# Attention outputs from split values and probabilities in fp32r, with sinks written by ScalarE

## The reference

```python
z = h @ w_in                                  # qa ka va | qb kb vb | forget gates
# sliding window, per head
m = max(max(s), sink); e = exp(s - m)
oa = (e / (sum(e) + exp(sink - m))) @ v
# forgetting, per head: F = cumsum(log sigmoid(gate))
s = q @ k.T * scale + F_q - F_k               # causal
ob = softmax(s) @ v
h = LN1(alpha * h + concat(oa, ob) @ w_o)
h = LN2(alpha * h + relu(h @ w_up)**2 @ w_down)
h = h + sigmoid(h @ w_pg + b_pg) * (p @ w_pe)
```

## Time and profile before

| | us |
|---|---|
| median of 3 runs (lowest, highest) | 2954.06 (2953.28, 2956.42) |
| the profiled execution | 2956.46 |
| its span | 2954.9 |
| PE busy | 2835.8 (96%) |
| DVE busy | 1244.1 (42%) |
| ACT busy | 856.9 (29%) |
| POOL busy | 120.6 (4%) |

### The profile page before, as it was taken

One profiled execution on the slowest core, in us unless ns is written; L12 is line 12 of the kernel. 1 busy time (PEld: TensorE's weight loads), 2 busy tenths in 40 slices (PEclk: granted clock), 3 DMA queues, 4 the chain that ended last, 5 costly groups with the idle time before them and its releaser, 6 DMA issues.

```text
span 2954.9 us, 51431 instructions
## 1 busy us (share of the span) xinstructions
PE 2835.8 (96%) x21021; PEld 2760.4 (93%) x21021; DVE 1244.1 (42%) x1759; ACT 856.9 (29%) x1377; POOL 120.6 (4%) x190
## 2 busy tenths in 40 slices
PE   7799999999899889999999999999999999998998
PEld 6688899999899889999999999999999999997998
DVE  7544443434634373333333333333333333355732
ACT  4344343434522162212222221222122112213511
POOL 0200121111100000000000000000000000000000
PEclk8899999999999999999999999999999999999999
DMA  4110122222122122222222222222222222222231
GB/s 166 46 36 29 59 85 79 74 73 81 62 65 77 64 80 79 86 80 86 86 76 82 86 86 86 86 73 86 87 79 86 79 86 81 83 74 63 87 110 52
DMA packets 65270, 230.72 MB, mean 78 GB/s; under 512 B 9280, under 2 KB 10176, under 8 KB 64576
## 3 DMA queue, kind: packets, MB, share of 16 engines
q1 hardware_dynamic: 57312, 211.31, 22.2%
q0 software_dynamic: 6160, 15.41, 1.6%
q10 hardware_dynamic: 1616, 1.18, 0.1%
HBM read 217.71 MB, written 10.16 MB: 77 GB/s over the span
## 4 chain that ended last, share of the span: by engine, by line
PE 92%; DVE 3%; issue 2%; ACT 2%; DMA 1%; ACTq 0%; DVEq 0%; POOL 0%; POOLq 0%
PE tile L354 81%; PE misc L519 3%; PE misc L354 3%; PE misc L499 1%; PE misc L463 1%; PE misc L462 1%; ACT w_hi L705 1%; DMA sv<-in_swa_cv 1%; DVE stat L1107 0%; PE misc L441 0%; PE tile L553 0%; PE misc L502 0%; PE misc L467 0%; DVE st L1041 0%; DVE acc L1035 0%
## 5 line engine op out<-in xcount | busy, mean ns | idle before, releaser
L354 PE MATMUL tile<-x_hi,w_hi 128*128 128x288 f32 (+1 forms) x4000 | 882.4, 302 | 37.5 <-DVE x_lo L1098 12.7
L354 PE MATMUL tile<-x_hi,w_lo 128*128 128x288 f32 (+1 forms) x4000 | 856.9, 296 | 0.0
L354 PE MATMUL tile<-x_lo,w_hi 128*128 128x288 f32 (+1 forms) x4000 | 856.6, 296 | 0.0
L354 PEld LDWEIGHTS tile<-x_hi,w_hi 128*128 128x128 f32 (+1 forms) x4000 | 640.3, 189 | 66.2 <-issue 54.8
L354 PEld LDWEIGHTS tile<-x_lo,w_hi 128*128 128x128 f32 (+1 forms) x4000 | 643.8, 189 | 1.2
L354 PEld LDWEIGHTS tile<-x_hi,w_lo 128*128 128x128 f32 (+1 forms) x4000 | 643.6, 189 | 1.3
L705 ACT ACTIVATE w_hi<-w_raw 128x1024 fp32r<-128x1024 f32 x394 | 406.3, 1052 | 637.5 <-PE tile L354 618.0
L1025 DVE TENSOR_TENSOR w_lo<-w_raw,w_hi 128x1024 fp32r<-128x1024 f32 x394 | 474.7, 1222 | 214.7 <-ACT w_hi L705 214.6
L354 PE MATMUL tile<-hid_hi,w_hi 128*128 128x288 f32 x2048 | 437.2, 295 | 7.9 <-DVE acc L1321 7.9
L354 PE MATMUL tile<-hid_lo,w_hi 128*128 128x288 f32 x2048 | 437.4, 294 | 0.0
L354 PE MATMUL tile<-hid_hi,w_lo 128*128 128x288 f32 x2048 | 434.5, 293 | 0.0
(11 more groups left out here) (216 smaller groups left out, 1956.5 us busy)
## 6 DMA issues: line engine op xcount, KB each, us to landing
w_raw<-in_w SPq DMA_DIRECT2D x394, 512.0 KB, 3.6
acc<-in_x SPq DMA_DIRECT2D x4, 1152.0 KB, 9.5
out_y<-st POOLq DMA_DIRECT2D x16, 288.0 KB, 2.6
out_fox_v<-v_t POOLq DMA_DIRECT2D x8, 288.0 KB, 2.4
out_fox_k<-k_t POOLq DMA_DIRECT2D x8, 288.0 KB, 2.4
c_t<-in_ck POOLq DMA_DIRECT2D x8, 256.0 KB, 3.0
c_v<-in_cv POOLq DMA_DIRECT2D x8, 256.0 KB, 2.9
p_raw<-in_p POOLq DMA_DIRECT2D x1, 576.0 KB, 4.0
```

The lines of the kernel that those rows point to most:

```text
L354: ins = nc.tensor.matmul(dst[:, h, :], w, x[:, h * HALF:(h + 1) * HALF], start=first and a == 0, stop=last and a == 2)
```

## The change

Values and transposed probabilities are split in two like the other operands. The stationary operand of the output product is a tile of 128 columns, 64 of high and 64 of low values of one head; it is multiplied by the high, then by the low probabilities. The result has 128 partitions, of which the lower and the upper half are added: ACT copies the upper half to SBUF, DVE adds the lower from PSUM and writes `acc`. Both heads of a pair use the same PSUM columns, so there are three such drains per pair (head 0, head 1, samples). ACT writes the sink into the score bank by a copy ahead of the scores. In `attend` ACT now copies the high probabilities before the exponential of the slot; DVE makes the low ones behind the normalisation. The forgetting pairs keep one buffer of high and one of low probabilities. The cached values are loaded to a spare row, earlier, and split in row 24. The row buffers are laid out anew (S1 and S2 apart), and their clearing stands behind the last operand of the output projection.

```diff
+def weighed_at(kind, j):
+    if kind == "swa":
+        return {9: [4], 10: [5], 11: [6], 12: [7, 8], 13: [9]}.get(j, [j - 4] if 4 <= j < 8 else [])
+    return [j - 4] if 4 <= j < SLOTS else []
+
+def drained_at(kind, j):
+    return {8 if kind == "swa" else 7: [0], 13 if kind == "swa" else 12: [1], 14: [2]}.get(j, [])
...
-        sv = sb("sv", [128, 6, 128], f32, swa)
-        s_pt = sb("s_pt", [128, 2, 256], f32, swa)
+        sv = sb("sv", [128, 6, 2, 128], f32r, swa)
+        s_ph = sb("s_ph", [128, 2, 256], f32r, swa)
+        s_pl = sb("s_pl", [128, 2, 256], f32r, swa)
...
-        f_pt = sb("f_pt", [128, 2, 512], f32, fox)
+        f_ph = sb("f_ph", [128, 1, 512], f32r, fox)
+        f_pl = sb("f_pl", [128, 1, 512], f32r, fox)
...
 PE, attend
+                    if kind == "swa":
+                        pe.wait_ge(sink_set, lin(g0 + j + 1, i, dg))
...
-                        ins = nc.tensor.matmul(scores_ps[:, end - 1:end], ident[:, :], sink_col(pair, head, i, dp),
-                                               start=True, stop=True)
...
-                    pe.wait_ge(turn_out, lin(g0 + s + 1, i, dg))
+                    pe.wait_ge(low_out, lin(g0 + s + 1, i, dg))
...
+                for s in weighed_at(kind, j):
+                    if s == 4:
+                        pe.wait_ge(out_free, lin(3 * pair + 2, i, 3 * dp))
...
+                    weigh(kind, s, ph, turn_out, True, lin(g0 + s + 2, i, dg))
+                    weigh(kind, s, pl, low_out, False, lin(g0 + s + 2, i, dg)).then_inc(weighed, 1)
+            def weigh(kind, s, probs, ready, first, count):
+                pe.wait_ge(ready, count)
+                dst = out_ps[:, 128 * qt:128 * qt + 128] if qt < 4 else \
+                    scores_ps[:, 512 + 64 * head:512 + 64 * head + 64]
+                for k, (vt, at) in enumerate(vals):
+                    keys = SAMPLE if qt == 4 and k == len(vals) - 1 else 128
+                    ins = nc.tensor.matmul(dst, vt[0:keys, at, head, :],
+                                           probs[0:keys, s % probs.shape[1], width * k:width * k + width],
+                                           start=first and k == 0, stop=not first and k == len(vals) - 1)
...
 ACT, attend
+                def drain():
+                    for d in drained_at(kind, j):
+                        act.wait_ge(weighed, lin(g0 + 2 + (4, 8, 10)[d], i, dg))
+                        act.wait_ge(out_free, lin(3 * pair + d + 1, i, 3 * dp))
+                        if d < 2:
+                            copy(low_half(pair)[:, 0:PROMPT], out_ps[64:128, :]).then_inc(half_out, 1)
+                        else:
+                            copy(low_half(pair)[:, 0:128], scores_ps[64:128, 512:640]).then_inc(half_out, 1)
+                if kind == "swa" or j != 7:
+                    drain()
+                if 3 <= j <= STEPS + 2:
+                    act.wait_ge(turned, lin(g0 + s + 3, i, dg))
+                    act.wait_ge(weighed, lin(g0 + s + (1 if kind == "swa" else 2), i, dg))
+                    copy(ph[:, s % ph.shape[1], 0:width], turn_ps[:, 0:width]).then_inc(turn_out, 1)
+                if kind == "swa" and j < STEPS - 1:
+                    act.wait_ge(exp_done, lin(g0 + j + 2, i, dg))
+                    set_sink(j + 1, pair, i, dp)
+                if kind == "swa" and j == STEPS and pair < PAIRS - 1:
+                    act.wait_ge(exp_done, lin(g0 + STEPS + 1, i, dg))
+                    set_sink(0, pair + 1, i, dp)
                 if j < STEPS:
                     ...
                     nc.scalar.activation(p[:, j % 4, 0:width], scores_ps[:, at:at + width], ACT.Exp, ...)
-                    copy(pt[:, s % 2, 0:width], turn_ps[:, 0:width]).then_inc(turn_out, 1)
+                if kind == "fox" and j == 7:
+                    drain()
...
 DVE, attend
+                if 3 <= j <= STEPS + 2:
+                    dve.wait_ge(turn_out, lin(g0 + s + 2, i, dg))
+                    V.tensor_tensor(pl[:, slot, 0:width], turn_ps[:, 0:width], ph[:, slot, 0:width], ALU.subtract).then_inc(low_out, 1)
+                for d in drained_at(kind, j):
+                    dve.wait_ge(half_out, lin(3 * pair + d + 1, i, 3 * dp))
+                    if d < 2:
+                        V.tensor_tensor(dst[64 * d:64 * d + 64, 0:PROMPT], out_ps[0:64, :], low_half(pair)[:, 0:PROMPT], ALU.add)\
+                            .then_inc(out_free, 1)
...
 values: ACT, then DVE (the same for sv, and for c_v in row 24)
-                copy(fv[:, 0:4, :], scores_ps[:, 0:512].rearrange("p (a b) -> p a b", a=4)).then_inc(fv_ready, 1)
+                copy(fv[:, 0:4, :, 0:64], turned_prompt()).then_inc(fv_hi, 1)
+                V.tensor_tensor(fv[:, 0:4, :, 64:128], turned_prompt(), fv[:, 0:4, :, 0:64], ALU.subtract).then_inc(fv_ready, 1)
...
 ACT, head
+            act.wait_ge(sv_ready, 2)
+            set_sink(0, 0)
...
 DVE, around the last pair
-            chain.add(V.memset(S1, 0.0))
-            chain.add(V.memset(S2, 0.0))
             dve.wait_ge(tile_done, T_O)
...
+            attend("fox", SLOTS, 2 * PAIRS - 1)
             operand_low(KT - 1)
+            chain.add(V.memset(S1, 0.0))
+            chain.add(V.memset(S2, 0.0))
...
 POOL
-                    pool.wait_ge(weighed, lin(2 + STEPS * (PAIRS + att), i, STEPS * dp))
+                    pool.wait_ge(cv_split, lin(att + 1, i, dp))
```

More of the change, by code:

```diff
@@ L174, in build @@
         lnv = sb("lnv", [128, 6, 5])
-        st = sb("st", [128, 5, TOK])
-        S1, S2, SH, WK = (st[:, k, :] for k in range(4))
-        WK2 = st[:, 4, :]
+        st = sb("st", [128, 3, TOK])
+        late = ExitStack()
+        sums = sb("sums", [128, 2, TOK], f32, late)
+        late.close()
+        S1, S2 = (sums[:, k, :] for k in range(2))
+        SH, WK, WK2 = (st[:, k, :] for k in range(3))
         MU, RSTD = S1, SH
         swa = ExitStack()
+        sq1 = sb("sq1", [128, 2, TOK], f32r, swa)
         win_r = sb("win_r", [128, 256], f32r, swa)
@@ L223, in build, with cached_values, low_half @@
         fox.close()
+        def cached_values(att):
+            raw = k_t[:, 0:512] if att == PAIRS - 1 else st[:, 1, 0:512]
+            return raw.rearrange("p (k h c) -> p k h c", k=4, h=2)
+        def low_half(pair):
+            return (v_t if pair == 2 * PAIRS - 1 else st[:, 0, :])[0:64, :]
         late = ExitStack()
+        late.enter_context(nc.sbuf_tensor("sums_home", [128, 2, TOK], f32))
         p_raw = sb("p_raw", [128, 2, TOK], f32, late)
@@ L732, in ln_apply @@
                         ahead.upto(u + 1 + c // 2)
-                    work = st[:, 3 + c % 2, :]
+                    work = st[:, 1 + c % 2, :]
                     act.wait_ge(ln_mul, KT * L + c + 1)
@@ L755, in attend, with set_sink @@
                                          bias=stat[:, s, 0:1], scale=1.0, accum_out=stat[:, s, 1:2]).then_inc(exp_done, 1)
[L756 to L770 removed]
+                if kind == "fox" and j == 7:
+                    drain()
+            def set_sink(j, pair, i=None, dp=0):
+                at, width = span("swa", j)
+                if j == 1:
+                    act.wait_ge(out_free, lin(3 * pair + 1, i, 3 * dp))
+                if i is not None:
+                    settle(act)
+                copy(scores_ps[:, at + width - 1:at + width], sink_col(pair, step_of(j)[0], i, dp)).then_inc(sink_set, 1)
             act.sem_inc(exp_done, 2)
             act.sem_inc(turn_out, 1)
[L774 removed]
             act.dma_start(ident_f[:, :], t["ident"]).then_inc(ident_landed, 16)
@@ L1004, in gate_tile @@
                 bias = cols[:, 6 * KT + kt:6 * KT + kt + 1] if i is None else cols[:, bass.ds(kt + 6 * KT, 1)]
-                nc.scalar.activation(halves(st[:, n % 2, :]), tile_ps(n), ACT.Sigmoid, bias=bias)\
+                nc.scalar.activation(halves(sums[:, n % 2, :]), tile_ps(n), ACT.Sigmoid, bias=bias)\
                     .then_inc(tile_free[n % 2], 1)
@@ L1103, in attend @@
                 p = s_p if kind == "swa" else f_p
+                ph, pl = (s_ph, s_pl) if kind == "swa" else (f_ph, f_pl)
                 if j < STEPS:
@@ L1270, in fox_pair @@
                             fox_queries(att, i, dp)
-                        for j in FOX_SLOTS.get(c, ()):
+                        if c == 2:
+                            fox_values(att, i, dp)
+                        for j in FOX_SLOTS.get(c, ()) if c != 46 else (SLOTS,):
                             attend("fox", j, PAIRS + att, i, dp)
+                        if c == 24:
+                            cached_low(att, i, dp)
                     if q is not None:
```

153 lines of the change are left out of this document (87 added, 66 removed).

## The result

The changed kernel takes 3020.07 us (median of 4; 3014.69 to 3030.32) against 2954.07: ratio 1.0224, interval 1.0198 to 1.0249. Slower, as forecast (the interval is clear of 1, though it holds 1.02), but +66 us where +34 was forecast, and 4 us outside the range. The profiled execution took 3030.3 (span 3028.0), +73.9 over the profiled execution of before; the comparison of traces goes by that execution, the longest of the four.

The account below looks back on a forecast made before the run. TensorE was taken to bound the kernel, with 92% of the chain of waits. Sliding-window pairs +10, head and pair 0 +6, forgetting +8, last pair +7, clock +3 gave +34: 2956.5 + 34 - 2.4 = 2988 us, range 2938 to 3016.

Parts of the forecast that it names:

- What PE saves: Attention pairs: sinks -11 us, switches between products -40, dearer sample steps +20; PE alone -31 us (-44 to -26).
- R4: Rival: weight loads of the new products are fast, 40 us less, partly eaten by sliding-window waits; near 2965 us, chance 0.03.
- What DVE and ACT get: Prices per new operation in the pairs: low parts 0.42 us for 256 columns, 0.69 for 512; sink copy 0.20; drain 0.59 plus 0.69.
- The waits: PE waits for step 7's low part at step 8: +1.6 or +2.5 us sliding-window, +2.0 forgetting; sliding-window step 9 +1.0.
- (a): Sliding-window pairs 1 to 7: step 4's product waits for the first drain, then PE for step 6's low part; together +0.7 us.
- +16, +8 and +7: Stage terms in us: pair 0 and sliding-window pairs +16 (+6 with the head, +10), forgetting pairs 0 to 6 +8, last pair +7.
- R1: Rival: DVE's and ACT's new work hides in idle time, no wait at step 8; 2923 us, or 2940 half hidden; chance 0.21.
- R2: Rival: the waits cancel the savings, net within 6 us of the kernel before, 2948 to 2960 us; chance 0.09.
- Clock: ... I take two such falls: +3.: TensorE's clock falls behind two of the new waits of 1.6 to 2.0 us in 14 pairs, 1.6 us each: +3.
- The bound of 14 x 1.6 = 22: Upper limit of the clock's cost in us: a fall behind the new wait in each of 14 pairs, 1.6 each.
- R3: Rival: the clock falls behind most new waits (+19 us), or GpSimd's collision comes in every pair (+6); 3013 us, chance 0.14.
- Everything after 850 us stays as it is: The change touches the 16 head pairs alone; the stages behind them, feed-forward included, were to change by 0.

Follow-up runs that it names:

- a4_fill: The changed kernel with filler products on TensorE ahead of step 8 in sliding-window and forgetting pairs, and 98 between pair 0's tile and the loop; 2995.5 us, ratio 1.0137.
- i_all: a4_fill with mean_w at 128 columns; 2980.3 us, ratio 1.009.
- a1_order: The changed kernel with sliding-window weight splits moved to row 5 and forgetting pairs' key splits to rows 36 and 39 on ScalarE and VectorE; 2977.7 us, ratio 1.0073.

## Why the prediction was wrong

By its steps:

1. *What PE saves* held. A sliding-window row went from 2.31 us to 1.81: 0.50 = 0.14 + 0.36; a prompt block of a forgetting pair became 0.32 shorter. The streaming pace stayed (0.12 a record), so R4 fell. The Trainium skill (TensorE: Matmul & The Clock Gate, section Weight-path perf modes) gives a fast load to types that are not FP32; nothing in these records shows one for fp32r. A forgetting sample block went from 0.86 to 1.47 us, +0.61 (0.7 forecast).
2. *What DVE and ACT get* held: 0.418, 0.684 and 0.682 us where 0.42, 0.69 and 0.69 stood; sink copies 0.17.
3. *The waits* were where they were put. At step 8 it was the higher price, with GpSimd's collision in six pairs, 2.33 to 2.36 (2.5), and 1.26 in pair 7; in forgetting pairs 1.5 to 2.3 (2.0); at step 9 0.89 (1.0). Only (a), the first drain, showed less: 0.23 at step 7's transposes. A pair without a fall of the clock became 1.0 us longer, 30.73 for 29.76 from the w_lo in row 0 of one tile to that of the next (1.5 forecast). The stages of a4_fill are +11.5, +7.5 and +7.5 us over the kernel before, 26.5 together, where +16, +8 and +7 stood. In the first two the clock falls no more than before. In the last pair it does, 0.84 for 0.92, some 11 us more at the lower level: that +7 came out as +7.5 is partly luck, since up to 5 of it (an estimate, half of those 11 us) is clock, which that term left out. R1 fell at the very place that was named for it, R2 by the time. For R1 the prediction also misread: VectorE does not idle over half of the last pair, it works 34.48 of 50 us.
4. *The step that failed: "Clock: ... I take two such falls: +3."* It cost 23, by a4_fill. Both the count and the price were too small. At step 8 the clock fell behind two of the six long waits of sliding-window pairs and five of seven in forgetting pairs, and it fell at both back edges too. The price stood at 1.6 us, from 3 us at the lower level behind 1.82; behind the 2.36 us at 184.6 the clock was 0.50 over 7 us and 0.55 over the next 7, and the two sliding-window pairs with a fall took 35.66 and 34.06 us from w_lo to w_lo, not 30.73: 4.9 and 3.3 for a fall. The bound of 14 x 1.6 = 22 was in the text and not believed; it comes near 23 by too many falls at too low a price. For pair 0's long wait nothing stood for the clock, though the wait of before already had 10 us at the lower level. R3 was the nearest case, and its 19 us for the clock the nearest price.
5. *"Everything after 850 us stays as it is"* failed: +17 in the feed-forward, 16 of it by the pace of products, which came back with the width of mean_w; the sum left the place of buffers out.
6. Nothing stood for *the back edges of the forgetting loop*: +8, by code that moved.

Together, in the profiled execution: waits 26.5 (the last pair's clock among them), clock 23, feed-forward 17, code 8, less 1.4 at the head and in the projection, 73. i_all takes out the clock of the first two stages, the buffers and the code: +25.7 us, the forecast's mechanism and nearly its size.

## What to carry to other kernels

Before an engine's new operation is called hidden, look at what stands ahead of it in that engine's order at the tightest place; here moving four splits a few rows turned +66 us into +24, and with the rest of the order, the places of buffers and code and fillers in one long wait into -17. Price a new wait on TensorE with the clock that may fall behind it, not with its length alone: behind waits of about 2 us it fell in half of the pairs here, for 3 to 14 us. And look at the granted clock again when a wait is gone; in a1_order's sliding window it was no higher. When a kernel loses time in a stage that no edit touches, compare the counts of instructions and the pace, and suspect addresses and the place of loops before the arithmetic.

## What the runs showed of the hardware

- The same 12332 products took 1688 or 1668 us when one buffer's width moved the others; 16 us of that is their pace. Down products took 0.1322 us each with the hidden rows at the place that they have in the kernel before or 384 bytes below it, 0.1333 at 448 or 480 below. Why is open; other places were not tried.
- A loop's back edge cost TensorE from nothing to 5.4 us by where its code stands. The Trainium skill (Runtime: NRT & Kernel Launch, section Instruction fetch mechanics) says that code comes in blocks of 16 KB and that a taken branch to code outside the held ones waits for a fetch. The traces agree in kind: packets of 16 KB on the instruction queue started about 4 us apart round these waits (at 518.3, 522.2 and 526.6 us round the one that ended at 524.86). In the kernel before they came as far apart round a wait of 1.52 us, so they do not explain the length. Which place is good was found by trial.
- After equal waits (2.34 and 2.36 us) the clock fell in some pairs and not in others, and in a1_order it fell at waits of 0.9 us; what tells them apart stays open.
